# Conditioned decoder trunk on one core: modulation sums by quarters, h by token halves, logits one step earlier

## The reference, cut to what matters

```python
c_act = silu(c)
mod = c_act @ w_ada[l] + b_ada[l]            # w_ada[l]: 1024 x 6144
sh_m, sc_m, g_m, sh_f, sc_f, g_f = split(mod, 6)
h = rmsnorm(x, norm_mix_g[l]) * (1 + sc_m) + sh_m
# layer 0: z = h @ w_in (1024 x 2560), gating MLP and short conv, y = ... @ w_out
# layer 1: causal pooling, y = ... @ w_pool * pool_scale
x = x + g_m * y
h = rmsnorm(x, norm_ffn_g[l]) * (1 + sc_f) + sh_f
g_logits, e_logits = h @ w_gr + b_gr, h @ w_er + b_er    # top group, top 2 experts in it
x = x + g_f * moe(h)
```

## Time and profile before

| | us |
|---|---|
| runs | 1816.09, 1817.61, 1818.15 (median 1817.61) |
| profiled execution | 1813.75 |
| its span | 1811.9 |
| TensorE busy | 1639.3 (90%) |
| VectorE busy | 1510.0 (83%) |
| ACT busy | 1030.9 (57%) |
| Pool busy | 437.1 (24%) |

### The profile page before, as it was taken

One profiled execution on the slowest core, in us unless ns is written; L12 is line 12 of the kernel. 1 busy time (PEld: TensorE's weight loads), 2 busy tenths in 40 slices (PEclk: granted clock), 3 DMA queues, 4 the chain that ended last, 5 costly groups with the idle time before them and its releaser, 6 DMA issues. The chain is left out here.

```text
span 1811.9 us, 20023 instructions
## 1 busy us (share of the span) xinstructions
PE 1639.3 (90%) x7847; PEld 1371.4 (76%) x7847; DVE 1510.0 (83%) x1095; ACT 1030.9 (57%) x840; POOL 437.1 (24%) x227
## 2 busy tenths in 40 slices
PE   3799999996899999999999949699999999999980
PEld 3577787785788888888888749678888888888870
DVE  5988785644699999999999758679999999999966
ACT  7221112322467777777777524357777777777742
POOL 1412130220424232322223100003432322233210
PEclk8799999997799999999999969789999999999995
DMA  9699712314699999999999954169999999999947
GB/s 340 203 314 314 266 69 81 119 46 197 218 343 376 381 385 390 385 383 387 381 388 388 387 210 173 49 234 365 381 388 387 387 383 384 384 384 387 386 183 285
DMA packets 125270, 547.62 MB, mean 302 GB/s; under 512 B 24003, under 2 KB 42975, under 8 KB 76021
## 3 DMA queue, kind: packets, MB, share of 16 engines
q1 hardware_dynamic: 91934, 497.98, 72.6%
q0 software_dynamic: 18432, 33.60, 4.9%
q10 hardware_dynamic: 14808, 14.73, 2.4%
HBM read 533.61 MB, written 46.17 MB: 320 GB/s over the span
## 5 line engine op out<-in xcount | busy, mean ns | idle before, releaser
L1310 DVE TENSOR_TENSOR unit_low<-unit,unit_high 128x2048 fp32r<-128x2048 f32 x384 | 856.0, 2283 | 15.3 <-ACT unit_high L924 15.0
L924 ACT ACTIVATE unit_high<-unit 128x2048 fp32r<-128x2048 f32 x384 | 735.4, 1915 | 42.6 <-DMA unit<-in_moe_w_up_dram 17.6
L1621 PE MATMUL ps<-unit_high,block_columns_high 128*128 128x512 f32 x1024 | 407.2, 398 | 10.4 <-DVE block_columns_low L1315 10.4
L714 POOL DMA_INDIRECT expert_rows<-y_out,assignment x64 | 214.8, 3357 | 804.3 <-DVE y_out L1340 791.9
L1623 PE MATMUL ps<-unit_high,block_columns_low 128*128 128x512 f32 x1024 | 401.2, 392 | 0.0
L1622 PE MATMUL ps<-unit_low,block_columns_high 128*128 128x512 f32 x1024 | 400.8, 391 | 0.0
L1621 PEld LDWEIGHTS ps<-unit_high,block_columns_high 128*128 128x128 f32 x1024 | 194.3, 190 | 50.2 <-DVE block_columns_low L1315 11.8
L1623 PEld LDWEIGHTS ps<-unit_high,block_columns_low 128*128 128x128 f32 x1024 | 193.5, 189 | 41.5
L1622 PEld LDWEIGHTS ps<-unit_low,block_columns_high 128*128 128x128 f32 x1024 | 193.8, 189 | 38.3
L1633 PE MATMUL ps<-unit_high,act_columns_high 128*128 128x512 f32 x512 | 206.7, 404 | 9.8 <-DVE unit_low L1310 9.8
L1635 PE MATMUL ps<-unit_high,act_columns_low 128*128 128x512 f32 x512 | 201.6, 394 | 0.0
(11 more groups left out here) (225 smaller groups left out, 1962.6 us busy)
## 6 DMA issues: line engine op xcount, KB each, us to landing
unit<-in_moe_w_gate_dram SPq DMA_DIRECT2D x128, 1024.0 KB, 7.7
unit<-in_moe_w_up_dram SPq DMA_DIRECT2D x128, 1024.0 KB, 7.3
unit<-in_moe_w_down_dram SPq DMA_DIRECT2D x128, 1024.0 KB, 8.5
cond_w<-in_w_ada_dram SPq DMA_DIRECT2D x80, 512.0 KB, 5.2
y_in<-expert_rows SPq DMA_DIRECT2D x16, 1024.0 KB, 7.3
x_rows<-in_x_dram SPq DMA_DIRECT2D x8, 1024.0 KB, 9.9
cond_w<-in_w_ada_dram SPq DMA_DIRECT2D x8, 1024.0 KB, 11.1
in_w<-in_w_in_even_dram ACTq DMA_DIRECT2D x12, 512.0 KB, 7.9
```

What stands on the lines that cost most here:

```text
L714: g.indirect_dma_start(out=y_dram[l], out_offset=bass.IndirectOffsetOnAxis(ap=index, axis=0), in_=src[:, :], in_offset=None, bounds_check= ...
L924: a.activation(high[k][:, :], raw[i % SLOTS][:, :], ACT.Copy).then_inc(unit_high, 1)
L1310: v.tensor_tensor(low[i % SLOTS][:, :], raw[i % SLOTS][:, :], high[k][:, :].bitcast(F32), ALU.subtract)\
L1621: mm(dst, xT_hi[:, q, :], high[k][:, cols], start=q == 0, stop=False)
```

## The change

Four things:

1. **Modulation sums.** The ten parts become three "quads" of 4, 4 and 2 parts. A chunk is still 128 x 1024, but holds 32 rows of `w_ada` for each of four parts, one part per quarter of the partitions (64 rows for each of two in the last quad). It comes by four (two) DMAs. VectorE adds 32, 32 and 16 chunks into `acc[n]`; a 128 x 4 (128 x 2) matrix of ones and zeros (`pick`) adds up each quarter, and one VectorE instruction on 4 (2) partitions multiplies all rows by their gains. The matrices of `c_act` columns for this come from six small DMAs on ACT's queue. There are five slots, not four. The sums stand behind units 13, 21 and 24. SP stores the rows; layer 0's gates are loaded back, broadcast.
2. **h in halves.** ACT, VectorE and TensorE work on 512 tokens at a time; ACT modulates odd blocks in place, VectorE does the even ones and all low parts; Pool has no part. VectorE makes the low parts of the first two pieces.
3. **Order of units.** The first two pieces are done on the first half of the tokens, then both on the second.
4. **Logits.** The logits of tile k - 2 go ahead of the transposes of tile k - 1.

```diff
-        CONDS = 4
-        PARTS = [(0, m) for m in range(2, NMOD)] + [(1, m) for m in range(NMOD)]
-        PART_BEHIND = {4 + 9 * n // 4: n for n in range(len(PARTS))}
+        QUADS = [(0, 2, 4), (1, 0, 4), (1, 4, 2)]
+        QUAD_BEHIND = {13: 0, 21: 1, 24: 2}
+        CONDS = 5
...
+        ORDER = [(0, 0), (1, 0), (0, 1), (1, 1)] + [(w, half) for w in range(2, PIECES) for half in range(2)]
...
+            def quad_loads(n, i):
+                l, m0, parts = QUADS[n]
+                rows = P // parts
+                for j in range(parts):
+                    sp.dma_start(acc[n][j * rows:j * rows + 1, :], b_ada[l:l + 1, (m0 + j) * D:(m0 + j + 1) * D])\
+                      .then_inc(bias_loaded, 16)
+                for g in range(D // rows):
+                    if i >= CONDS:
+                        sp.wait_ge(cond_used, i - CONDS + 1)
+                    for j in range(parts):
+                        sp.dma_start(cond[i % CONDS][j * rows:(j + 1) * rows, :],
+                                     w_ada[l, g * rows:(g + 1) * rows, (m0 + j) * D:(m0 + j + 1) * D])\
+                          .then_inc(cond_loaded[i % CONDS], 16)
+                    i += 1
...
+            for n, (l, m0, parts) in enumerate(QUADS):
+                sp.wait_ge(row_out, n + 1)
+                sp.dma_start(mod_dram[l][m0:m0 + parts, :], mod_rows[n][0:parts, :]).then_inc(row_stored, 16)
+            sp.wait_ge(part_summed, len(QUADS))
...
+            for i, m in enumerate((G_M, G_F)):
+                sp.dma_start(grow[i][:, :], mod_dram[0][m].partition_broadcast(P)).then_inc(gain0_loaded, 16)
...
+            for half in range(2):
+                tokens = slice(half * CH, (half + 1) * CH)
+                for b in range(KD // 2):
+                    for k in (2 * b, 2 * b + 1):
+                        a.activation(h_hi[:, k, tokens], hT[:, k, tokens], ACT.Identity, scale=a_m[:, k:k + 1],
+                                     bias=mod_c[:, SH_M, k:k + 1]).then_inc(h_act, 1)
+                    if half == 0 and b == 0:
+                        piece_high(1)
+                    act.wait_ge(h_act, 12 * half + 3 * b + 2)
+                    a.activation(hT[:, k, tokens], hT[:, k, tokens], ACT.Identity, scale=a_m[:, k:k + 1],
+                                 bias=mod_c[:, SH_M, k:k + 1]).then_inc(h_act, 1)
...
+            for half in range(2):
+                tokens = slice(half * CH, (half + 1) * CH)
+                for b in range(KD // 2):
+                    k = 2 * b
+                    dve.wait_ge(h_act, 12 * half + 3 * b + 1)
+                    v.tensor_scalar(hT[:, k, tokens], hT[:, k, tokens], a_m[:, k:k + 1], mod_c[:, SH_M, k:k + 1],
+                                    ALU.mult, ALU.add).then_inc(h_dve, 1)
+                    if b:
+                        dve.wait_ge(h_act, 12 * half + 3 * b)
+                        h_rest(k - 1, half)
+                    dve.wait_ge(h_dve, 4 * half + b + 1)
+                    h_rest(k, half)
...
+                for g in range(D * parts // P):
+                    dve.wait_ge(cond_loaded[i % CONDS], 16 * sum(PARTS_OF[i % CONDS:i + 1:CONDS]))
+                    ch.link(v.scalar_tensor_tensor(out=acc[n][:, :], in0=cond[i % CONDS][:, :],
+                                                   scalar=c_of[parts][:, g:g + 1], in1=acc[n][:, :],
+                                                   op0=ALU.mult, op1=ALU.add))
...
+                for half in range(2):
+                    last = mm(ROWS[n % 2][0:parts, half * CH:(half + 1) * CH], pick[parts][:, :],
+                              acc[n][:, half * CH:(half + 1) * CH], start=True, stop=True)
...
-            for k in range(NT + 2):
+            for k in range(NT + 1):
...
+                if 0 <= k - 2:
+                    entry_logits(0, k - 2)
                 if 0 <= k - 1 < NT:
                     entry_T(0, k - 1)
-                if 0 <= k - 2:
-                    entry_logits(0, k - 2)
+            entry_logits(0, NT - 1)
```

More of the change, by code:

```diff
@@ L476, in _ @@
             sp.dma_start(ws_raw[:, :, :], w_spatial[0].rearrange("h t s -> t h s")).then_inc(ws_loaded, 16)
[L478 to L488, removed]
+            def quad_loads(n, i):
[12 more added lines that the diff above has]
+                    i += 1
+                return i
             for l in range(LAYERS):
@@ L630, in _ @@
             g.sem_inc(consts, 1)
+            for i, tile in enumerate((pick4, pick2)):
+                note(g.memset(tile[:, :], 0.0))
+            for tile in mod_rows:
+                note(g.memset(tile[:, :], 1.0))
+            settle()
+            for parts in (4, 2):
+                for j in range(parts):
+                    rows = P // parts
+                    note(g.memset(pick[parts][j * rows:(j + 1) * rows, j:j + 1], 1.0))
+                settle()
             pool.wait_ge(x_T, NT)
-            for q in range(2):
-                note(g.memset(bias[q][:, :], 0.0))
+            for tile in acc:
+                note(g.memset(tile[:, :], 0.0))
             settle()
@@ L799, in piece_high @@
                 a.activation(piece_hi[w % HRING][:, :, :], piece[w % RING][:, :, :], ACT.Copy).then_inc(w_high, 1)
+            piece_high(0)
             act.wait_ge(mod_ready0, 1)
[L803 to L811, removed]
@@ L1093, in conv @@
+            i = 0
+            for n in range(len(QUADS)):
+                i = quad_sum(n, i)
+                if n:
+                    quad_rows(n - 1)
+            quad_rows(len(QUADS) - 1)
             def conv(m):
@@ new lines, in project @@
+                if u >= 4:
+                    done = u - 3
+                    pe.wait_ge(*((proj_kept, done) if done <= 6 * KA else (z_kept, done - 6 * KA)))
+                tokens = slice(half * CH, (half + 1) * CH)
+                for k in range(KD):
+                    if u in (0, 2):
+                        pe.wait_ge(h_low, half * KD + k + 1)
+                    w_hi, w_lo = piece_hi[w % HRING][:, k, :], piece_lo[w % RING][:, k, :]
+                    mm(BANK[u % 4], w_hi, h_hi[:, k, tokens], start=k == 0, stop=False)
+                    mm(BANK[u % 4], w_hi, h_lo[:, k, tokens], start=False, stop=False)
+                    last = mm(BANK[u % 4], w_lo, h_hi[:, k, tokens], start=False, stop=k == KD - 1)
@@ L1531, in _ @@
+                last.then_inc(proj_done, 1)
+                if u in QUAD_BEHIND:
+                    sum_quad(QUAD_BEHIND[u])
             pe.wait_ge(x_T_kept, NT)
             pe.wait_ge(mod_ready0, 1)
[L1533 to L1534 removed]
+            for u in range(2 * PIECES):
+                project(u)
             pe.wait_ge(ws_loaded, 16)
[L1537 removed]
+            pe.wait_ge(row_out, len(QUADS))
             for h in range(HEADS):
```

207 lines of the change are left out of this document (80 added, 127 removed).

## The result

The changed kernel takes **1853.86 us** (median of 4 runs, 1845.25 to 1857.77), the kernel before 1817.88 (4 runs, 1816.09 to 1819.05): ratio 1.0192, 95% interval 1.0151 to 1.0234. So it is 36 us slower, where 1806 was forecast; the range given, 1790 to 1848, misses it by 6. The profiled execution took 1850.31 us, its span is 1848.6.

The account below looks back on a forecast made before the run. Two chains were taken to end together near 220 us: TensorE's units and the 80 chunk sums. Terms -10.8 + 1.5 - 2.0 = -11.3 us gave 1802.5 against the profiled execution, 1806 us by the median; range 1790 to 1848.

Parts of the forecast that it names:

- The step that failed: Chunk loads before VectorE's sums: a DMA wait of 0.10 us per chunk, so 1.84 us a chunk in all.
- The formula built round it: Whole time as 1817.6 - 220 + (62 + 80 r) - 0.5 = 1659 + 80 r, with r the time per chunk.
- The second rival: DMA between SP's issue and VectorE's sum: quarter loads are slow, 1828 to 1884 us, some 1845; chance 0.30.
- SP's issues: SP's chunk loads: 0.30 to 0.34 us per quarter, 1.2 to 1.35 us for four; SP not the bound.
- First chunk sum at 60.4: End of making h on VectorE: the first chunk sum starts at 60.4 us, 2 us earlier than before.
- First projection matmul at 44.5, four units done near 69.5: TensorE's early projections: start near 44.5 us, four units end near 69.5 where they ended at 84.7.
- Pool's collisions: VectorE's chunk sums beside Pool's in_w_low subtractions: 0.31 us per chunk, as before the change.
- TensorE waits 9 and 12 us for the second and third sum: TensorE's quad sums: idle 9 and 12 us before the second and third, released by VectorE.
- The same 39.85 us after the last sum: TensorE from the last sum to the spatial transposes: needs the same 39.85 us as before.
- 380 GB/s and more from 432 us on: Expert stages from 432 us on: DMA rate of 380 GB/s and more, nothing edited, only starting earlier or later.
- Logits, -2.0: Last tile: tile 7's logits start at 434.9 us, not 437.0, with tile 6's ahead of the wait, 2.0 us gained.
- TensorE's lead: Projections: TensorE gains a lead of 15 us from its earlier start, worth only what the chunk chain allows.

Follow-up runs that it names:

- e2: The changed kernel with each chunk loaded by one DMA over 128 partitions (80 DMAs, not 288), holding other rows than the sums mean: 1803.21 us, ratio 0.9915.
- by_rows: The changed kernel with each chunk's 32 rows read as (row, part) in one load over 128 partitions, and c in two loads: 1802.85 us, ratio 0.9915.
- loads-only kernel: A separate kernel, only loads of w_ada in eight forms, one after the other: quarters 240 GB/s, halves 243, whole and row-wise loads 408 to 415.
- latest-sums kernel: The by_rows kernel with the sums behind units 14, 23 and 26 of the projections, not 13, 21 and 24: 1794.11 us, ratio 0.9879.

## Why the prediction was wrong

**The step that failed** is the price of the loads: "I take a DMA wait of 0.10 per chunk, the 0.15 of before less a little for the fifth slot". It measured 69.3 / 80 = 0.87 us; less the usual gap, which the prediction left out of its 0.15 (3.5 us of 15.5 in 28 waits, so 8 us in 64), 0.77. The formula built round it comes within 4 us: with the 1.75 us per chunk of e2, 1659 + 80 r gives 1799 (measured 1803), with by_rows' 1.77 it gives 1801 (1803), and with the changed kernel's (255.2 - 64.4) / 79 = 2.415 us it gives 1852 (1854). That is in part luck, since the first sum, 4.0 us later than forecast, and the logits, worth nothing for 2.0, aren't in it, and the 1.6 us of a quad row is counted twice when r is measured so. The sums' own loads in 4 KB rows were taken as the nearest row to the new ones, but they were near in the length of a row and far in what the runs with whole, half and by_rows loads show to count: whether one load fills all 128 partitions.

**The second rival** came true in size and place: DMA waits over 40 us, landings of 8.1 us, r above 2.03. Its mechanism is half right. The slow packets in full engines are as it said; that three quarters lie idle meanwhile is too simple, since halves, of which two in flight could cover everything, ran at the same 239 to 243 GB/s. What held its chance down to 0.30 was the argument that four quarters are in flight together, and the loads-only kernel shows that this helps little (217 for one alone, 240 in order, 268 to 284 alternating).

Point by point:
- *SP's issues*, forecast 0.30 to 0.34 us for a quarter: 0.42 by median, so 1.7 for a chunk. Still under the 2.4 of a chunk and hidden here; it would not have been beside the 1.43 of a sum.
- *First chunk sum at 60.4*: 64.43. The terms given add up to 59.9, not 60.4. The start cost 2.5 us, for which the prediction charged nothing: half for the six small loads of c, with the columns at 9.45 us instead of 5.34, half for TensorE's slower sums over the partitions. The stage of h itself took 20.0 us and not 17.3, since ACT, with 24 operations of 0.8 us, sets its pace and not VectorE.
- *First projection matmul at 44.5, four units done near 69.5*: 47.03 and 73.6; 46.18 with by_rows.
- *Pool's collisions* at 0.31 us per chunk: 23.2 / 80 = 0.29 with by_rows. Right.
- *TensorE waits 9 and 12 us for the second and third sum*: 6.3 and 6.0 with by_rows; 33.25 and 15.29 in the changed kernel.
- *The same 39.85 us after the last sum*: in the changed kernel the shift of the sum, 36.74, is that of the span. Right. With by_rows the sum is 14.85 earlier and the first expert unit 13.2 (457.1 for 470.3).
- *380 GB/s and more from 432 us on*: a misreading; slices 11 to 13 of the earlier trace rows have 218, 343 and 376, and a second dip follows at slice 24. Nothing in the sum hangs on it.
- *Logits, -2.0*: nothing that can be measured, for the reason above.
- *TensorE's lead "is worth only what the chunk chain allows"*: right, both ways. It hid nothing of the slow loads.

## What to carry to other kernels

A DMA share near 1 says that the engines are busy, not that they move much: read it beside the GB/s of the same window. Keep a load on all 128 partitions in one DMA; where a sum needs several parts on the partitions, change the mapping of partitions (row-major over the parts) so that one load still fills them. And price a changed load by the row that shares its span of partitions; where no row does, that is the largest uncertainty of the forecast.

## What was not expected of the hardware

**VectorE stands still beside a long Pool subtraction.** In the kernel before and in all the others but the last, two sums of the convolution that take 1.30 us each elsewhere take 13.27 or 13.28 together. VectorE and Pool of the by_rows kernel:

```profile
227.52 13.28 DVE L1115 SCALAR_TENSOR_TENSOR conv_out<-conv_in,vector_columns,conv_out 128x1023 f32<-128x1023 f32 x2
...
244.20 2.60 DVE L1115 SCALAR_TENSOR_TENSOR conv_out<-conv_in,vector_columns,conv_out 128x1023 f32<-128x1023 f32 x2
```

```profile
230.66 9.05 POOL L658 TENSOR_TENSOR v_w_low<-v_w,v_w_high 128x4096 fp32r<-128x4096 f32 x1 [0.90 <-ACT v_w_high L843]
```

Pool's one subtraction lies inside, and the pair is 10.7 us longer than usual. In the latest-sums kernel the two engines meet at another place, and there another instruction is the long one, which takes 1.23 us elsewhere:

```profile
220.76 2.60 DVE L1115 SCALAR_TENSOR_TENSOR conv_out<-conv_in,vector_columns,conv_out 128x1023 f32<-128x1023 f32 x2
...
223.40 9.92 DVE L1118 TENSOR_TENSOR mix_b<-mix_b,conv_out 128x1024 f32<-128x1024 f32 x1
```

```profile
222.23 10.01 POOL L658 TENSOR_TENSOR v_w_low<-v_w,v_w_high 128x4096 fp32r<-128x4096 f32 x1 [2.06 <-ACT v_w_high L843]
```

So the delay goes with Pool's subtraction and not with the instruction, and it fits the chunk sums drawn out to 3.4 us beside Pool's shorter ones. No run without that subtraction was made.

**The expert stage differs from profile to profile.** From the first expert unit to the last router matmul of layer 1 the profiled execution before took 685.7 us (470.3 to 1156.0); the others took 691.6 (halves of h), 689.5 (by_rows), 689.0 (logits) and 685.5 (latest sums), with nothing edited in it. Each is one execution. That is as large as the gains of single edits, so small ones were read from medians and from the start of the first unit, and not from spans.

**Repeating each value is slow for its size.** VectorE's two copies that spread c, 32 and 16 partitions with 128 elements each, took 1.93 us together.
